# A two-block network on one Trainium2 core: the mixture-of-experts router laid on four column tiles, its counting in two products, and the first expert weights loaded and split ahead of the gathered tokens

## The reference

```
logits = xt @ router                         # 256 x 1024 @ 1024 x 8
top_logit, top_e = lax.top_k(logits, 2)
gates = softmax(top_logit)
# assignments sorted by expert, padded to blocks of 128 rows
y[token] += gate * (silu(x_blk @ w_gate[e]) * (x_blk @ w_up[e])) @ w_down[e]   # D_FF_EXPERT = 3584
```

## Time and profile before

| | |
|---|---|
| runs of the kernel before | 2996.67 us median of 3 (2996.46, 2996.67, 3004.22) |
| the profiled execution, first to last instruction (span) | 3000.9 us; its time as the runs are timed is not given apart, the span lies inside the range of the runs |
| PE busy | 2781.2 us (93%) |
| DVE busy | 1939.4 us (65%) |
| ACT busy | 1475.5 us (49%) |
| POOL busy | 67.4 us (2%) |
| mean granted TensorE clock | 0.961 of full speed |
| routing and opening of the experts | about 1277 to 1321 us of the span |

### The profile page before, as it was taken

How to read it: one execution, slowest core, us unless ns; L and a number is a source line. 1 busy time by engine, 2 the same in 40 slices (tenths; PEclk the granted TensorE clock), 3 DMA queues, 4 the chain that set the end, 5 groups by cost and what they waited for, 6 DMA issues and landing times.

```text
span 3000.9 us, 50779 instructions
## 1 busy us (share of the span) xinstructions
PE 2781.2 (93%) x21394; PEld 2331.0 (78%) x21394; DVE 1939.4 (65%) x2283; ACT 1475.5 (49%) x1746; POOL 67.4 (2%) x44
## 2 busy tenths in 40 slices
PE   6987878999989978879999999999999889998999
PEld 4864766888768758768787787877877779996999
DVE  3356765222443567468888888888888557665665
ACT  3235233222333342357776777777776445453543
POOL 1100000000002000010000000000000000000000
PEclk9999998999999989779999999999999889998999
DMA  7225201222223340069898998989997424542453
GB/s 305 94 98 218 101 3 57 98 98 87 96 85 113 118 184 4 2 229 359 335 371 332 349 352 335 372 337 354 358 348 273 158 92 170 189 155 75 153 185 113
DMA packets 81460, 581.70 MB, mean 194 GB/s; under 512 B 9064, under 2 KB 10736, under 8 KB 11504
## 3 DMA queue, kind: packets, MB, share of 16 engines
q1 hardware_dynamic: 78192, 571.49, 50.6%
q10 hardware_dynamic: 3072, 7.33, 0.7%
HBM read 577.73 MB, written 1.05 MB: 193 GB/s over the span
## 4 chain that ended last, share of the span: by engine, by line
PE 53%; DVE 5%; PEld 2%; ACT 2%; issue 1%; DMA 0%; PEldq 0%; DVEq 0%; ACTq 0%; POOLq 0%; POOL 0%; SPq 0%
PE banks L2538 20%; PE banks L2562 10%; PE banks L953 8%; PE banks L987 3%; PE banks L2928 3%; PEld banks L642 2%; PE banks L1605 2%; DVE ring_split L2715 1%; DVE x_buf L2704 1%; PE banks L2548 1%; PE banks L2575 1%; DVE arena L1098 0%; PEld banks L2117 0%; PE banks L2117 0%; PE banks L3006 0%
## 5 line engine op out<-in xcount | busy, mean ns | idle before, releaser
L2715 DVE TENSOR_TENSOR ring_split<-ring,arena_split 128x2048 fp32r<-128x2048 f32 x336 | 768.4, 2291 | 91.4 <-ACT arena_split L2643 83.3
L2643 ACT ACTIVATE arena_split<-ring 128x2048 fp32r<-128x2048 f32 x336 | 644.4, 1919 | 52.7 <-PE banks L2562 52.7
L305 DVE TENSOR_TENSOR ring_split<-ring,arena_split 128x2048 fp32r<-128x2048 f32 x144 | 334.1, 2322 | 325.7 <-ACT arena_split L299 325.7
L2538 PE MATMUL banks<-arena_split 128*128 128x512 f32 x896 | 301.7, 399 | 11.7 <-DVE ring_split L2715 11.7
L299 ACT ACTIVATE arena_split<-ring 128x2048 fp32r<-128x2048 f32 x144 | 274.4, 1908 | 75.4 <-PE banks L1165 74.0
L2538 PE MATMUL banks<-arena_split,mix_split 128*128 128x512 f32 x896 | 303.3, 401 | 6.4 <-DVE ring_split L2715 6.4
L2562 PE MATMUL banks<-arena_split 128*128 128x512 f32 x896 | 297.4, 392 | 1.0 <-DVE arena_split L2744 1.0
L2538 PEld LDWEIGHTS banks<-arena_split 128*128 128x128 f32 x896 | 169.6, 189 | 49.2 <-DVE ring_split L2715 13.4
L2538 PEld LDWEIGHTS banks<-arena_split,mix_split 128*128 128x128 f32 x896 | 168.4, 188 | 45.2 <-DVE ring_split L2715 8.3
L2562 PEld LDWEIGHTS banks<-arena_split 128*128 128x128 f32 x896 | 168.1, 188 | 43.5 <-issue 4.4
L953 PE MATMUL banks<-mix_split,ring_split 128*128 128x256 f32 x704 | 198.7, 282 | 0.0
(11 more groups left out here) (386 smaller groups left out, 5406.7 us busy)
## 6 DMA issues: line engine op xcount, KB each, us to landing
ring<-parts SPq DMA_DIRECT2D x541, 1024.0 KB, 4.8
arena<-bias ACTq DMA_DIRECT2D x2, 2048.0 KB, 8.7
x_buf<-xt SPq DMA_DIRECT2D x1, 2048.0 KB, 13.1
constants<-con SPq DMA_DIRECT2D x1, 2026.0 KB, 8.3
out<-x_buf ACTq DMA_DIRECT2D x1, 1024.0 KB, 4.8
arena<-lora ACTq DMA_DIRECT2D x2, 256.0 KB, 2.7
arena<-gate ACTq DMA_DIRECT2D x2, 256.0 KB, 4.2
arena<-sgw ACTq DMA_DIRECT2D x2, 256.0 KB
```

The lines of the kernel that those rows point to most:

```text
L305: dve.tensor_tensor(low_slots[:, n % RING, :], slots[:, n % RING, :], high[:, m % high.shape[1], :].bitcast(F32), ALU.subtract).then_inc(w ...
L2538: mm = pe.matmul(pair_bank(U), x[:, k, at], w[:, j, :], start=k == 0 and g == 0, stop=k == KT - 1 and g == 2)
L2643: act.activation(high[:, m % 3, :], slots[:, m % RING, :], ACT.Copy).then_inc(wh_ok.h, 1)
L2715: dve.tensor_tensor(low_slots[:, m % RING, :], slots[:, m % RING, :], high[:, m % 3, :].bitcast(F32), ALU.subtract).then_inc(wl_ok.h, 1)
```

## The change

- **Router on column tiles, folded.** The router's weights are padded from 8 to 32 columns per chunk (the load grows from 32 KB to 128 KB) and become the stationary operand; the 256 tokens move. Four chunks go at once, each on its own 32 of the array's 128 columns; two such rounds, after the 4th and after the 8th shifted chunk, leave four partial sums on the partitions of bank 6. ACT copies them out (new step `lr`), and two products with the constant `fold8` add the four sums and turn them to tokens x experts (step `lg`). These two stand on PE between the transposes `t0` and `t1`.
- **Counting in two products.** `ones` and `before` are each multiplied once with `sel` of both halves. DVE adds what the products did before (`first`, `total`, `before0`, `before1`), and `passes` is now made ahead of `key`.
- **Experts' opening.** SP waits for the step `passes` of DVE instead of the end of the phase. On ACT and on DVE the splits of weight parts 0 and 1 stand ahead of the gathered tokens, part 2 stays behind.

```
--- before.py
+++ after.py
@@ -62,7 +62,7 @@
...
-                  ("before", 128), ("slot", 128), ("fold", 4)]:
+                  ("before", 128), ("slot", 128), ("fold", 4), ("fold8", 8)]:
     CON[_name] = (_at, _at + _n)
     _at += _n
 CON_COLS = _at
@@ -116,6 +116,7 @@
...
     put("fold", ((p[:, None] // 64 == np.arange(4)[None, :] // 2) & (p[:, None] % 32 == np.arange(4)[None, :] % 2)) * 1.0)
+    put("fold8", (p[:, None] % 32 == np.arange(8)[None, :]) * 1.0)
...
@@ -2299,33 +2300,40 @@
         tok_high, tok_low = a.take_split(2 * D, 2), a.take_split(2 * D, 2)
         at = a.at
 
-        rt = a.take(KT * N_EXP, KT)
+        rt, lrows = a.take(KT * 32, KT), a.take(LAT)
         W = lambda: a.take(2 * N_EXP, 2)
         lg, v1, o1, v2, o2, l2, sel = (W() for _ in range(7))
         st = [a.take(2, 2) for _ in range(8)]
-        cnt = a.take(2)
+        cnt, first, total = a.take(2), a.take(N_EXP), a.take(N_EXP)
         rin, shifted = S("router_loaded"), S("norm_shifted")
 
         @block.scalar
         def _(act):
-            act.dma_start(rt, router_in[:, :].rearrange("p (k e) -> p k e", e=N_EXP)).then_inc(rin.h, 16)
+            act.dma_start(rt, router_in[:, :].rearrange("p (k e) -> p k e", e=32)).then_inc(rin.h, 16)
         V_ = Steps(S("route_dve"), ["lg"] + [f"{x}0" for x in ("m", "v", "w", "x", "o")] + ["l2"] +
                    [f"{x}1" for x in ("m", "v", "w", "x", "o")] + ["dif", "sel", "one", "inv", "g2", "s0", "s1", "s2",
-                                                                 "key0", "key1", "cnt0", "cnt1", "passes", "tok0", "tok1"])
-        A_ = Steps(S("route_act"), ["t0", "e", "t1"])
-        P_ = Steps(S("route_pe"), ["lg", "t0", "t1", "pos"])
+                                                                 "first", "total", "before0", "cnt0", "before1", "cnt1",
+                                                                 "passes", "key0", "key1", "tok0", "tok1"])
+        A_ = Steps(S("route_act"), ["lr", "t0", "e", "t1"])
+        P_ = Steps(S("route_pe"), ["lr", "t0", "lg", "t1", "pos"])
         iota = con[:, CON["iota"][0]:CON["iota"][1]]
 
         @block.tensor
         def _(pe):
             pe.wait_ge(rin.h, 16)
-            for k in range(KT):
-                pe.wait_ge(shifted.h, shifted.at(k + 1))
-                for tt in range(2):
-                    mm = pe.matmul(bank(6 + tt)[:, 0:8], hT[:, k, CTX + tt * P:CTX + (tt + 1) * P], rt[:, k, :],
-                                   start=k == 0, stop=k == KT - 1)
-            mm.then_inc(P_.h, P_.one("lg"))
+            for r in range(2):
+                pe.wait_ge(shifted.h, shifted.at(4 * r + 4))
+                for j in range(4):
+                    k = 4 * r + j
+                    mm = pe.matmul(bank(6)[32 * j:32 * j + 32, 0:LAT], rt[:, k, :], hT[:, k, CTX:T],
+                                   start=r == 0, stop=r == 1, tile_position=(0, 32 * j))
+            mm.then_inc(P_.h, P_.one("lr"))
             for tt in range(2):
+                if tt:
+                    pe.wait_ge(A_.h, A_.at("lr"))
+                    for i in range(2):
+                        mm = pe.matmul(bank(7)[:, 8 * i:8 * i + 8], lrows[:, i * P:(i + 1) * P], C("fold8"), start=True, stop=True)
+                    mm.then_inc(P_.h, P_.one("lg"))
                 for k in range(KT):
                     b = 2 + 2 * tt + k // 4
                     mm = pe.transpose(bank(b)[:, (k % 4) * P:(k % 4 + 1) * P], hT[:, k, CTX + tt * P:CTX + (tt + 1) * P],
@@ -2333,11 +2341,9 @@
                 mm.then_inc(P_.h, P_.one(f"t{tt}"))
             pe.wait_ge(V_.h, V_.at("sel"))
 
-            pe.matmul(bank(1)[:, 0:8], C("before"), sel[:, 0, :], start=True, stop=True)
-            pe.matmul(bank(1)[:, 8:16], C("ones"), sel[:, 0, :], start=True, stop=False)
-            pe.matmul(bank(1)[:, 8:16], C("before"), sel[:, 1, :], start=False, stop=True)
-            pe.matmul(bank(1)[:, 16:24], C("ones"), sel[:, 0, :], start=True, stop=False)
-            pe.matmul(bank(1)[:, 16:24], C("ones"), sel[:, 1, :], start=False, stop=True).then_inc(P_.h, P_.one("pos"))
+            pe.matmul(bank(1)[:, 0:16], C("ones"), sel.rearrange("p t e -> p (t e)"), start=True, stop=True)
+            pe.matmul(bank(0)[:, 0:16], C("before"), sel.rearrange("p t e -> p (t e)"), start=True, stop=True)\
+                .then_inc(P_.h, P_.one("pos"))
 
         @block.scalar
         def _(act):
@@ -2346,6 +2352,8 @@
                 act.wait_ge(normed.scaled.h, normed.scaled.at(k + 1))
                 y = hT[:, k, CTX:T]
                 act.activation(y, y, ACT.Identity, bias=normed.shift(k, 1)).then_inc(shifted.h, shifted.one())
+            act.wait_ge(P_.h, P_.at("lr"))
+            act.activation(lrows, bank(6)[:, 0:LAT], ACT.Copy).then_inc(A_.h, A_.one("lr"))
             act.wait_ge(P_.h, P_.at("t0"))
             act.activation(tok_high[:, 0, :], banks[:, 2 * 512:4 * 512], ACT.Copy).then_inc(A_.h, A_.one("t0"))
             act.wait_ge(V_.h, V_.at("dif"))
@@ -2361,7 +2369,7 @@
             for k in range(KT):
                 normed.scale(dve, k, hT)
             dve.wait_ge(P_.h, P_.at("lg"))
-            dve.tensor_copy(lg, v3(banks[:, 6 * 512:8 * 512], 2)[:, :, 0:8]).then_inc(V_.h, V_.one("lg"))
+            dve.tensor_copy(lg, v3(bank(7)[:, 0:16], 2)).then_inc(V_.h, V_.one("lg"))
 
             def pick(i, src, v, o):
 
@@ -2395,21 +2403,26 @@
             dve.tensor_tensor(gate, v1, v2, ALU.add).then_inc(V_.h, V_.one("s2"))
 
             dve.wait_ge(P_.h, P_.at("pos"))
-            dve.scalar_tensor_tensor(key, v3(bank(1)[:, 0:16], 2), 1.0, sel, ALU.add, ALU.mult)\
-                .then_inc(V_.h, V_.one("key0"))
+            dve.tensor_copy(first, bank(1)[:, 0:8]).then_inc(V_.h, V_.one("first"))
             dve.wait_ge(V_.h, V_.s.m)
-            dve.tensor_scalar(key, key, 1.0, None, ALU.subtract).then_inc(V_.h, V_.one("key1"))
-
-            dve.tensor_reduce(cnt[:, 0:1], bank(1)[:, 16:24], AX.X, ALU.max).then_inc(V_.h, V_.one("cnt0"))
-            dve.wait_ge(V_.h, V_.s.m)
+            dve.tensor_tensor(total, bank(1)[:, 8:16], first, ALU.add).then_inc(V_.h, V_.one("total"))
+            dve.tensor_copy(key[:, 0, :], bank(0)[:, 0:8]).then_inc(V_.h, V_.one("before0"))
+            dve.wait_ge(V_.h, V_.at("total"))
+            dve.tensor_reduce(cnt[:, 0:1], total, AX.X, ALU.max).then_inc(V_.h, V_.one("cnt0"))
+            dve.tensor_tensor(key[:, 1, :], bank(0)[:, 8:16], first, ALU.add).then_inc(V_.h, V_.one("before1"))
+            dve.wait_ge(V_.h, V_.at("cnt0"))
             dve.tensor_scalar(cnt[:, 1:2], cnt[:, 0:1], P + 0.5, 1.0, ALU.is_gt, ALU.add).then_inc(V_.h, V_.one("cnt1"))
             dve.wait_ge(V_.h, V_.s.m)
             dve.tensor_copy(passes[:, :], cnt[:, 1:2]).then_inc(V_.h, V_.one("passes"))
+            dve.scalar_tensor_tensor(key, key, 1.0, sel, ALU.add, ALU.mult).then_inc(V_.h, V_.one("key0"))
+            dve.wait_ge(V_.h, V_.s.m)
+            dve.tensor_scalar(key, key, 1.0, None, ALU.subtract).then_inc(V_.h, V_.one("key1"))
 
             for tt in range(2):
                 dve.wait_ge(A_.h, A_.at(f"t{tt}"))
                 dve.tensor_tensor(tok_low[:, tt, :], banks[:, (2 + 2 * tt) * 512:(4 + 2 * tt) * 512],
                                   tok_high[:, tt, :].bitcast(F32), ALU.subtract).then_inc(V_.h, V_.one(f"tok{tt}"))
+        counted = V_.at("passes")
         end_phase()
 
 
@@ -2481,7 +2494,7 @@
 
         @block.sync
         def _(sp):
-            sp.wait_ge(S("phase_met").h, 4 * phase["n"])
+            sp.wait_ge(V_.h, counted)
             sp.wait_ge(used.h, stream["put"])
             with sp.Fori(0, passes_of(sp)) as p:
                 def load(n, i=None, wait_for=None):
@@ -2681,11 +2694,12 @@
 
                 def own_part(e, u):
                     pass
+                for m in range(2):
+                    split(m, 0)
                 gathered_out(0, 0, 4)
                 gathered_out(0, 1, 6)
                 sent_out(0)
-                for m in range(3):
-                    split(m, 0)
+                split(2, 0)
                 for e in range(N_EXP):
                     over_units(act, e, body, own_part)
                 sums_out(N_EXP - 1)
@@ -3495,7 +3510,9 @@
         b = i["na_rpb"][l][:, r_at, np.clip(c_at, 0, 30)]
         b = np.where(near, b, np.float32(0))
         bias.append(b.reshape(NA_H, 2, P, LAT).transpose(2, 1, 0, 3).reshape(P, -1))
-    router = i["moe_router"][0].reshape(KT, P, N_EXP).transpose(1, 0, 2).reshape(P, KT * N_EXP)
+    router = np.zeros((P, KT, 32), np.float32)
+    router[:, :, 0:N_EXP] = i["moe_router"][0].reshape(KT, P, N_EXP).transpose(1, 0, 2)
+    router = router.reshape(P, KT * 32)
     sgw = i["sg_w_2"].transpose(0, 3, 1, 2).reshape(DEPTH, P, 4 * P)
     arrays = {
         "parts": np.stack(parts), "xt": xt, "ct": ct, "con": constants(), "par1": np.stack(par1), "par2": np.stack(par2),
```

78 lines of the change are left out of this document (48 added, 30 removed).

## The result

| | before | changed |
|---|---|---|
| median of 21 runs each | 2997.63 us | 3007.45 us |
| lowest to highest | 2991.1 to 3008.53 | 2998.47 to 3012.96 |
| span of the profiled execution | 3000.9 us | 3000.4 us |
| mean granted clock in it | 0.961 | 0.971 |

The changed kernel is **slower**, by 9.8 us in the medians: ratio 1.0023, 95% interval 1.0014 to 1.0033. That is little, but clear of no change. Forecast was 0.21% faster. The profiled execution of the change is one of its fastest (3002.13 us as a run), so the two spans must not be compared as wholes; the stretches in them can be.

What follows compares the result with a forecast made beforehand. PE bounds the kernel through the experts' units, so only the way to the first unit counts: 3.3 us earlier start plus 3.0 from the clock make 6.3 us off the median 2996.67, giving 2990.4 us, range 2987.0 to 2996.5.

Steps and rivals of the forecast that it cites:

- The step that failed: Experts' units: PE sets their pace, untouched by the change, so only time off the way to the first unit counts.
- The slower rival (2): Experts' opening: weight splits queued ahead of gathered tokens on ACT and DVE delay `product(0)` if loads land late; 2999.0, chance 0.04.
- Rival 3: Router: tiles do not overlap with large moving operands, or the fold waits; everything moves 4.3 us, 2994.7, chance 0.04.
- Rival 4: Routing phase: the clock rises, transposes and fold halve (1.3 us), and DVE meets no collision; 2988.8, chance 0.1.
- Rival 1: First gate and up pair: the clock gives nothing, only the 3.3 us stay; 2993.4, chance 0.27.
- logits copied: Router: tiles and fold give logits at 1288.3 instead of 1288.8, 0.5 us, no more, as the fold waits behind `t0`.
- first use of the exponential: Picks on DVE: ACT's copy of `t0` ends earlier, so the wait for the exponential goes and its successor starts 2.0 us sooner.
- `product(0)` starts: Experts' opening: first gate and up products start at 1308.8 instead of 1312.13, 3.3 us sooner, after DVE's splits and gathered low parts.
- hardly bind: Experts' opening: ACT's copies of gathered tokens, ready at 1306.1 or in the late bound 1307.5, hardly delay `product(0)`.
- The clock: First 24 products: PE idles 3.3 us instead of 5.0, so full clock, 5.3 us against 8.49, another 3.1 us (bounds 0 to 3.1).
- the 0.3 us that I took: Experts' opening: POOL's matrices collide with DVE's splits, which may start late by 0 to 1.2 us; 0.3 taken.
- The 4.1 us gap: Earlier trace: after 4.1 nearly idle us PE's clock was still full, taken as evidence for full clock after 3.3 us.

Runs made afterwards that it cites:

- pad8: The kernel before with eight unused columns (32 bytes) more behind the constants, so every buffer behind them moves: 3013.69 us, ratio 1.0048.
- arena_32: The kernel before with a gap of 32 unused bytes directly ahead of the arena, so that the arena alone moves: 3013.44 us, ratio 1.0056.
- In place: The whole change against the kernel before, fold8 loaded with the router into scratch space so every buffer keeps its address: 2994.4 us against 3000.73, ratio 0.9976.

## Why the prediction was wrong

**The step that failed** stands in its first paragraph: "PE sets that pace, and the change touches none of its units" and "From there the old and the new program run alike". They run the same instructions, but 32 bytes displaced, and these are not alike: the displacement alone costs 14 to 17 us in the medians of pad8 and arena_32, of which the profiles show 4.5 to 5.6 in the dense layer, about 2.5 in the first mixers and 4.0 in the units. The prediction priced `fold8`'s products and put the place of its constant at nothing, without a word on it; none of the four rivals named it. The slower rival (2) blamed weights standing in the queues' way; that did not happen.

**Rivals.** Rival 3 (no overlap of tiles) is out: 1.08 us per round. Rival 4's faster clock in the routing phase did come (the second eight transposes took 1.07 us against 1.97), after the logits were through, so it gave almost nothing. Rival 1 was half right, see the clock below.

**Step by step**, from the end of the last shift, changed kernel against before:

| step | forecast | measured |
|---|---|---|
| logits copied | 0.5 us sooner | 0.7 (3.6 for 4.4 us) |
| first use of the exponential | 2.0 | 2.2 (6.5 for 8.7) |
| tokens' low parts begin, phase ends | 1.6 | 1.9 (8.7 for 10.5) |
| first load issued | 4.2 | 4.5 |
| gather | as long as before, 5.6; at most 7.0 | 6.6 |
| `product(0)` starts | 3.3 | 3.9 (23.7 for 27.7) |
| `product(0)` length | 3.1 shorter | 1.1 shorter (7.4 for 8.5) |
| sum | 6.3 | 5.1 |

The first load landed 4.8 us after its issue as reckoned (1296.02 to 1300.84), the second 7.3 us after the same issue (reckoned 7.7). What bound the start was not DVE's splits: they were done at 1307.56, and DVE had made the first low part by 1308.70. It then waited 0.32 us for ACT's copy of the second half, which could begin only at 1307.96, when the gather was through. The gather ran its first 5.7 us at the lower clock, before only 3.3. It stayed inside its bound of 7.0 us, but the prediction's "hardly bind" for that case was wrong by these 0.32 us.

**The clock** was the mis-sized term. PE stood for only 1.9 us and the clock was still full in that gap, yet the first nine products ran at 0.53. In the kernel with the opening alone the gap was 3.3 us, as forecast, the first products were fast, and then the clock fell while PE was busy; there too the 24 products took 7.3 us:

```profile
1299.70:1302.80 3.10, 0.00 (x0) 0.00 (x0) 3.10 (x4) 3.08 (x5) 2.98 (x4) 1.00 1.02 428
1302.90:1303.90 1.00, 1.00 (x5) 0.84 (x6) 1.00 (x1) 0.60 (x1) 0.00 (x0) 1.00 0.97 410
1304.00:1307.30 3.30, 3.30 (x10) 2.54 (x9) 0.94 (x1) 0.00 (x0) 0.00 (x0) 0.50 0.20 82
```

I had asked only how long PE idles, and a full clock at the end of the gap did not carry through the products. The trace of the kernel before could have shown this. The 4.1 us gap that I took as a good sign was followed by the lower clock too, half a microsecond after PE had begun again. And the 5.1 us gap from 2326.90 on the earlier trace rows, which I took as the cause of a low clock, was not: the clock had fallen before it, while PE was busy, behind an earlier gap (before 2323.20) in which it was full:

```profile
1109.20:1109.70 0.50, 0.50 (x32) 0.50 (x36) 0.34 (x1) 0.00 (x0) 0.00 (x0) 1.00 0.89 377
1109.80:1115.00 5.20, 4.34 (x106) 4.15 (x99) 2.78 (x6) 0.00 (x0) 0.00 (x0) 0.50 1.01 425
...
2320.70:2323.10 2.40, 0.00 (x0) 0.00 (x0) 1.28 (x1) 1.04 (x1) 0.00 (x0) 1.00 0.00 0
2325.00:2326.80 1.80, 1.80 (x8) 1.58 (x8) 1.30 (x4) 0.00 (x0) 0.00 (x0) 0.50 0.00 0
```

So this term gave 1.1 us, not 3.1.

**POOL beside DVE.** Two groups of four matrices took 4.30 and 4.25 us, not 2.33 each, while DVE's splits began within 0.03 us of their inputs and took 2.29 us as ever. In each group one matrix was held up (2.57 and 2.51 us instead of 0.60); POOL waited, DVE didn't, and the 0.3 us that I took were not paid. The Trainium skill (SBUF — State Buffer, Who interferes with whom) says that the one that issues first blocks the other. The trace agrees for the matrices: each of the two began 0.2 to 0.3 us after a split had, and ended only behind it. It does not show the other direction: the first split began at 1302.78, while POOL was in a matrix begun at 1302.39, and did not wait; but spans on POOL are rough.

**The size, with the fault removed.** In place, the change is faster by 6.3 us in the medians (0.9976), the forecast 6.3. That the number agrees is partly luck: the traces show 5.1 to 5.5 us, the interval of the ratio reaches from 4 to 11 us, and the forecast had the clock's part 2 us too large and the start of `product(0)` 0.6 us too late.

## What to carry to other kernels

When a change adds a constant or resizes a buffer, look at what is allocated behind it, and hold every address still while you measure the rest; a kernel with the same padding and no other change is the control. When the whole is slower, compare stretches of unchanged code between the two traces by first and last start of a line: stretches of dense products repeated within 0.7 us here, mostly 0.3, while whole runs spread by more than 10. Look at the granted clock of a stretch before its length is put down to anything else. And tile positions are worth a sweep of their own: modulo 256 bytes they were worth over twice the change itself.

## What the hardware showed that was not expected

- The time of PE's products of 512 columns with operands split in SBUF depends on where the tiles lie, by their remainder by 256 bytes: medians of 388 to 398 ns in the profile, 240.5 to about 247.5 us for the dense stretch (up to 248.6 with more time at the lower clock) and 981.6 to 998.0 for the experts' units, wholly at 2.4 GHz. +256 bytes gave the old stretches back.
- The best of the positions tried was the same in both stages, remainder 128 for all tiles that the products read. In the experts' units, +192 bytes for the weights' high halves alone cost 5 us, for all tiles it gave 10.
- A product's own two operands don't settle its time: with the same addresses it had a median of 389 ns in one kernel and 393 in another, and with neither operand moved it went from 393 to 398.
- The second block's products of 256 columns were slowest with their tiles at remainder 128 (283 against 280 ns), so there is no one good position for all shapes. Why any of this is so stays open: no run looked at single accesses, and whether PE's two reads meet each other, or the reads and writes of ACT, DVE and DMA take part, was not tried.
- TensorE's clock can fall from 2.4 to 1.2 GHz while products are running, soon after a gap during which it had still been full: 1.0 us after the products had begun in the kernel with the opening alone (gap 3.3 us), and about 0.1 us after in the changed one (gap 1.9 us).
